# A layer with expert lookup on one core: the gates of the first token of each group of eight multiplied as high and low part

## The chip, the cores and the metric

The kernel runs on one core of a Trainium2 chip. The metric is the time of one execution on the device in microseconds. Times of single runs stand beside one profiled execution, in which every instruction has its start and duration.

## What is computed

One transformer layer for 256 tokens and 16 meta tokens, model width 1024: an input projection, sparse attention beside a pooling mixer, an output projection, and then the part that matters here, a product-key expert layer (PEER). Each token has 8 heads; each head picks 16 experts out of 128 x 128 with a softmax gate:

```python
    eid = jnp.take_along_axis(cand_i, pos, axis=-1)
    gate = jax.nn.softmax(top_s, axis=-1)
...
        a = jnp.einsum('td,tkd->tk', hb, peer_u[eb], preferred_element_type=jnp.float32)
        a = jax.nn.gelu(a, approximate=False)
        return jnp.einsum('tk,tkd->td', (gb * a).astype(hb.dtype), peer_v[eb])
```

So a token has 128 chosen experts, each with an index pair (i1, i2) and a gate.

## The kernel before

The kernel does not gather experts. It computes the products of all tokens with all 16,384 experts, in 128 blocks of 128, and multiplies them by a dense table of gates `gates[i2, i1, token]` that is zero where a token did not choose the expert. The stages are: the projections and attention (to about 150 us), the queries, the search for the best keys and the first "early" expert products (to about 254 us), the table of gates (about 259 to 340 us), and then 128 blocks in a steady rhythm of `up` and `down` products (to the end). The heavy products are made from float32 values split into a high and a low part in the type float32r, which TensorE takes in one pass; three such products (high x high, high x low, low x high) stand for one exact one. Products of plain float32 operands are called native here; TensorE shows two records (weight load and matmul) for each of them, and one for each single-pass product.

**The gate stage** is what the change touches. For one token the 128 x 128 table of gates is one product over its 128 choices: a one-hot matrix of one index against a one-hot matrix of the other index, each row of the latter multiplied by the choice's gate. Tokens are taken in 32 groups (NQ) of eight (GRP), q = 0 to 31, through OHS = 3 rotating slots:

- VectorE, `ones` (L1059): both one-hot matrices of eight tokens, by one comparison of 128 x 2048 elements against a row of numbers. It waits until TensorE has done group q - 3 (`b_done`).
- ScalarE, `gated` (L619), takes the first two tokens (ACT_T = 2): it multiplies the one-hot of 128 x 128 by the token's column of gates in `picks[:, 2]`, as the activation's scale, and writes plain float32 into `oh_g`. GpSimd, `gated` (L1277), does the same for the other six in one operation.
- TensorE, `gate_group` (L1574): waits for both (`ohg_up`, `ohp_up`) and for the copy of the slot's last results (`b_ev`), and makes eight native products of 128 x 128 x 128 into two banks of PSUM.
- ScalarE, `keep_gates` (L624): copies 128 x 1024 results into the table. It waits for `b_done` of that group, so in ScalarE's queue it stands behind the gated one-hots of the next group.

In the same stage seven more early expert products (13 to 19) are made by `split_part` (L1581) between the gate groups: a period of EARLY_Q = 4 groups holds 9 products after the group with q = 1 mod 4, 9 after q = 2 mod 4 and 6 after q = 3 mod 4. Each needs a block of expert weights split in halves: high part by ScalarE (`early_hi`, L636), low part by GpSimd (`early_lo`, L1285), and its result goes through a gelu on ScalarE (`early_gelu`, L566). The order of ScalarE's queue is written out by hand: in each iteration q the gated one-hots of q, then the copy of group q - 1; behind that, for q = 3 mod 4, the first half block, and for q = 0 mod 4 the gelu and the second half block. GpSimd takes its share of group q and then its half block (q = 0 and 1 mod 4). From q = 28 on no half blocks are left; at q = 29 ScalarE instead splits the first full block of the following stage (L560). The memory of the one-hots, `oh`, ends at element 8D of the row `rr` (D = 1024), and the last D elements, `g_sp`, are used only once all groups are done.

Of the kernel before, what the change touches and what calls it, by code (L numbers as in the profile page):

```python
# [8 lines left out]
ALU = mybir.AluOpType  # L9
ACT = mybir.ActivationFunctionType  # L10
AX = mybir.AxisListType
ds = bass.ds

P = 128
SEQ, META = 256, 16
T = SEQ + META
D = 1024
# [6 lines left out]
NK = 128  # L24
PH, TOPK = 8, 16
GRP = 8
NQ, OHS = SEQ // GRP, 3
# [4 lines left out]
ACT_T = 2  # L32
# [57 lines left out]
def layer(nc, x, meta, w_in, gq, gk, pool_w, w_out, wq, sk1, sk2, pu, pv, const, out):  # L90
    ctx = ExitStack()
    with ctx:
        def sb(name, shape, dt=F32):
            return ctx.enter_context(nc.sbuf_tensor(name, shape, dt))

        def sem(name):
            return ctx.enter_context(nc.semaphore(name))
# [4 lines left out]
        rr = sb("rr", [P, 9 * D], F32R)  # L102
# [4 lines left out]
        picks = sb("picks", [P, 3, SEQ])  # L107
        gel = sb("gel", [P, 2, SEQ])
        psum = ctx.enter_context(nc.psum_tensor("psum", [P, 8, 512], F32))
# [98 lines left out]
        ut = [rr[:, n:n + 2 * D].rearrange("p (a k n) -> p a k n", a=2, k=DK) for n in (0, 4 * D)]  # L208
        v_sp = [rr[:, n:n + 2 * D].rearrange("p (a d) -> p a d", a=2) for n in (6 * D, 2 * D)]
        oh = rr[:, 2 * D:8 * D].rearrange("p (s a q n) -> p s a q n", s=OHS, a=2, q=GRP)  # L210
        g_sp = rr[:, 8 * D:9 * D].rearrange("p (s a t) -> p s a t", s=2, a=2)

        def f(ap):
            return ap.bitcast(F32)
# [30 lines left out]
        ld_e = [sem(f"ld_e{s}") for s in range(2)]  # L245
        ld_v3 = sem("ld_v3")
        d_place, n_ev, ld_iota, a_root = sem("d_place"), sem("n_ev"), sem("ld_iota"), sem("a_root")
        d_inv, p_table = sem("d_inv"), sem("p_table")
        d_rel, p_qk = sem("d_rel"), sem("p_qk")
        p_cand, p_cide = sem("p_cand"), sem("p_cide")  # L250

# [33 lines left out]
        def early_bank(e):  # L285
            return (2, 5)[e % 2] if e < EARLY_TOP - 1 else 0
# [119 lines left out]
        def _(act):  # L406
# [155 lines left out]
            def early_gelu(e):  # L562
                act.wait_ge(e_up, e + 1)
                if e >= 2:
                    act.wait_ge(st_e[e % 2], 16 * (e // 2))
                act.activation(gel[:, e % 2, :], psum[:, early_bank(e), 0:SEQ], ACT.Gelu).then_inc(e_gel, 1)  # L566
# [45 lines left out]
            act.activation(picks[:, 0:2, :].rearrange("p a t -> p (a t)"), psum[:, 6, :], ACT.Copy).then_inc(pk_ev, 1)  # L612
            act.wait_ge(pe_pk, 2)
            act.activation(picks[:, 2, :], psum[:, 7, 0:SEQ], ACT.Copy).then_inc(pk_ev, 1)
            early_gelu(EARLY_TOP - 2)

            def gated(s, tok):
                for j in range(ACT_T):
                    i = act.activation(oh_g[:, s, j, :], f(oh[:, s, 1, j, :]), ACT.Copy, scale=picks[:, 2, ds(tok + j, 1)])  # L619
                i.then_inc(ohg_up, 1)  # L620

# [3 lines left out]
                   .then_inc(b_ev, 1)  # L625

            act.wait_ge(pk_ev, 2)

            def early_hi(j, half):
                e, ks = EARLY_TOP + j, slice(half * DK // 2, (half + 1) * DK // 2)  # L630
                act.wait_ge(ld_u[e % 2], 16 * (e // 2 + 1))
                if j and half == 0:
                    act.wait_ge(e_half, j)
                elif j:
                    act.wait_ge(e_up, e)
                act.activation(ut[0][:, 0, ks, :], u_raw[:, e % 2, ks, :], ACT.Copy).then_inc(e_hi, 1)  # L636

            for q in range(NQ):
                act.wait_ge(oh_up, q + 1)
                gated(q % OHS, GRP * q)  # L640
                if q == 1:
                    early_gelu(EARLY_TOP - 1)
                    early_hi(0, 0)
                    early_hi(0, 1)
                if q:
                    act.wait_ge(b_done, q)
                    keep_gates((q - 1) % OHS, GRP * q - GRP)
                if q % EARLY_Q == EARLY_Q - 1 and EARLY_TOP + q // EARLY_Q + 1 < EARLY:
                    early_hi(q // EARLY_Q + 1, 0)
                if q and q % EARLY_Q == 0 and EARLY_TOP + q // EARLY_Q - 1 < EARLY:  # L650
                    early_gelu(EARLY_TOP + q // EARLY_Q - 1)
                    if EARLY_TOP + q // EARLY_Q < EARLY:
                        early_hi(q // EARLY_Q, 1)
                if q == NQ - 3:
                    block_u(0, EARLY, 8 * EARLY + 16, True)
# [47 lines left out]
        def _(dve):  # L703
# [232 lines left out]
            for c in range(OUT0, WQ0):  # L936
                for t in range(2):
                    dve.wait_ge(z_done, z_after(c) - 1 + t)
                    n = (c - OUT0) * CW
# [118 lines left out]
            def ones(s, tok):  # L1058
                dve.tensor_tensor(oh[:, s], iota_in.unsqueeze(1).unsqueeze(1).to_broadcast([P, 2, GRP, NK]),  # L1059
                                  picks[:, 0:2, ds(tok, GRP)].unsqueeze(3).to_broadcast([P, 2, GRP, NK]), ALU.is_equal)\  # L1060
                   .then_inc(oh_up, 1)
# [3 lines left out]
            for q in range(NQ):  # L1065
                if q >= OHS:
                    dve.wait_ge(b_done, q - OHS + 1)
                ones(q % OHS, GRP * q)


            def block_v(s, b):
# [54 lines left out]
            for t in range(2):  # L1126
# [4 lines left out]
                for n in range(2):  # L1131
                    a = t * D + n * 512
# [163 lines left out]
        def _(pe):  # L1296
# [238 lines left out]
            for h in range(PH + 1):  # L1535
# [6 lines left out]
                if h != 2:  # L1542
                    g = h if h < 2 else h - 1
# [24 lines left out]
            def gate_group(q, s, first=False):  # L1568
                pe.wait_ge(ohg_up, q + 1)
                pe.wait_ge(ohp_up, q + 1)  # L1570
                if not first:
                    pe.wait_ge(b_ev, q - OHS + 1)
                for j in range(GRP):
                    i = pe.matmul(psum[:, 2 + 2 * s + j // 4, (j % 4) * P:(j % 4 + 1) * P], f(oh[:, s, 0, j, :]), oh_g[:, s, j, :],  # L1574
                                  start=True, stop=True)
                i.then_inc(b_done, 1)
# [12 lines left out]
            for q in range(NQ):  # L1589
                gate_group(q, q % OHS, q < OHS)  # L1590
                j, part = q // EARLY_Q, q % EARLY_Q
                e = EARLY_TOP + j
                if e < EARLY and part:
                    if part == 1:
                        pe.wait_ge(e_gel, e)
                    pe.wait_ge(e_lo, 2 * j + min(part, 2))
                    i = split_part(e, EARLY_K[part - 1], EARLY_K[part])
                    if part == 2:
                        i.then_inc(e_half, 1)
                    if part == 3:  # L1600
                        i.then_inc(e_up, 1)
# [92 lines left out]
```

## Time and profile before

| | us |
|---|---|
| median of 3 runs | 1002.54 |
| lowest and highest run | 1001.08, 1002.66 |
| the profiled execution | 1002.49 |
| its span, first to last instruction | 1000.5 |
| TensorE matmuls busy in the span | 978.5 |
| VectorE, ScalarE, GpSimd busy | 677.5, 442.3, 184.5 |

The profile names instructions by engine (PE is TensorE's matmul, PEld its weight loads, DVE VectorE, ACT ScalarE, POOL GpSimd, SP the queue of the loads and stores) and by the line of the kernel. TensorE's clock is granted in full in every slice of the span. Matmuls are pipelined, so their durations overlap: the distance from one start to the next is what a product costs, not the mean duration of one. Idle time in brackets stands behind an instruction that had to wait, with what released it.

### The profile page before, as it was taken

To read this page: it belongs to the slowest core of one execution; us is meant where nothing else is said; L and a number is where in the kernel's file an instruction comes from. 1 tells how busy PE (TensorE), PEld (TensorE's weight loads), DVE (VectorE), ACT (ScalarE), POOL (GpSimd) and SP (SyncE) were. 2 spreads that over 40 slices of the span, in tenths; PEclk is the share of its full clock that TensorE was granted. 3 is DMA by queue.
4 is the path that set the end of the run, shared out by engine and by line. 5 is a ranking of instruction groups with operands and counts; after the bars stand their busy time and mean duration, and the time that the engine had idled before them with its cause. 6 is when DMAs were issued, how large, how long until landed. Compare 5 with 4: busy or idle time off the path is not lost.

```text
span 1000.5 us, 18315 instructions
## 1 busy us (share of the span) xinstructions
PE 978.5 (98%) x6396; PEld 890.4 (89%) x6396; DVE 677.5 (68%) x1266; ACT 442.3 (44%) x698; POOL 184.5 (18%) x228
## 2 busy tenths in 40 slices
PE   7999899999999999999999999999999999999998
PEld 7898798887999878999999999999999999999997
DVE  5697737789888788565656565656565656565655
ACT  5555532212677633444444444444444444444442
POOL 3273304787678300000000000000000000000000
PEclk9999999999999999999999999999999999999999
DMA  7532136414412577545555555454555454555454
GB/s 243 180 119 96 56 114 206 142 56 141 121 54 80 161 237 244 185 170 206 172 207 170 207 171 206 171 206 170 207 173 205 172 205 171 199 179 206 171 203 151
DMA packets 69585, 168.34 MB, mean 168 GB/s; under 512 B 6688, under 2 KB 35488, under 8 KB 69552
## 3 DMA queue, kind: packets, MB, share of 16 engines
q1 hardware_dynamic: 68080, 167.47, 49.3%
q10 hardware_dynamic: 1472, 0.44, 0.2%
q8 instruction: 20, 0.33, 0.1%
q14 instruction: 13, 0.11, 0.0%
HBM read 163.16 MB, written 4.72 MB: 168 GB/s over the span
## 4 chain that ended last, share of the span: by engine, by line
PE 93%; DVE 3%; DMA 2%; ACT 1%; POOL 1%; issue 1%; DVEq 0%
PE psum L1311 38%; PE psum L1616 34%; PE psum L1574 6%; PE psum L1488 6%; PE psum L1524 4%; PE psum L1581 2%; DMA raw<-in_peer_u_dram 1%; PE psum L1518 1%; PE psum L1343 1%; POOL big L1196 1%; PE psum L1435 1%; PE psum L1303 0%; DVE big L750 0%; DVE big L873 0%; DMA cst<-in_const_dram 0%
## 5 line engine op out<-in xcount | busy, mean ns | idle before, releaser
L1616 PE MATMUL psum<-rr 128*128 128x512 f32 x1536 | 369.3, 391 | 1.1 <-issue 0.7
L1311 PEld LDWEIGHTS psum<-h_all,rr 128*128 128x128 f32 x2688 | 331.0, 188 | 8.9 <-DVE big L873 0.5
L1311 PE MATMUL psum<-h_all,rr 128*128 128x256 f32 (+1 forms) x2688 | 334.0, 280 | 0.1
L1616 PEld LDWEIGHTS psum<-rr 128*128 128x128 f32 x1536 | 280.7, 188 | 56.2 <-issue 0.9
L1073 DVE TENSOR_TENSOR rr<-raw,rr 128x1024 fp32r<-128x1024 f32 x109 | 133.5, 1225 | 215.5 <-ACT rr L664 215.5
L664 ACT ACTIVATE rr<-raw 128x1024 fp32r<-128x1024 f32 x109 | 115.6, 1061 | 287.2 <-PE psum L1616 287.2
L560 ACT ACTIVATE rr<-raw 128x1024 fp32r<-128x1024 f32 x108 | 114.6, 1061 | 54.6 <-DMA raw<-in_peer_u_dram 54.6
L1012 DVE TENSOR_TENSOR rr<-raw,rr 128x1024 fp32r<-128x1024 f32 x108 | 131.6, 1219 | 1.1 <-ACT rr L560 0.9
L1311 PE MATMUL psum<-rr,h_all 128*128 128x256 f32 (+1 forms) x672 | 81.3, 281 | 2.5 <-ACT raw L476 1.5
L1311 PEld LDWEIGHTS psum<-rr,h_all 128*128 128x128 f32 (+1 forms) x672 | 77.6, 175 | 5.5 <-issue 1.9
L1059 DVE TENSOR_TENSOR rr<-psum,picks 128x2048 fp32r<-128x2048 f32 x32 | 72.4, 2288 | 9.5 <-PE psum L1574 7.7
L1574 PE MATMUL psum<-raw,rr 128*128 128x128 f32 x512 | 62.9, 277 | 1.1 <-ACT raw L619 0.9
L1574 PEld LDWEIGHTS psum<-raw,rr 128*128 128x128 f32 x512 | 59.8, 192 | 2.7 <-ACT raw L619 2.1
L1088 DVE TENSOR_TENSOR rr<-big,rr 128x256 fp32r<-128x256 f32 x128 | 54.5, 426 | 4.4
L1488 PE MATMUL psum<-big 128*128 128x256 f32 x256 | 56.7, 379 | 0.0
L1082 DVE TENSOR_TENSOR big<-big,gel 128x256 f32 (+1 forms) x128 | 53.5, 418 | 4.5 <-ACT big L624 4.5
L1488 PEld LDWEIGHTS psum<-big 128*128 128x128 f32 x256 | 48.3, 190 | 6.4
L1277 POOL TENSOR_TENSOR raw<-rr,picks 128x768 f32<-128x768 f32 x32 | 47.9, 1499 | 21.7 <-DVE rr L1059 21.7
L1524 PE MATMUL psum<-big,raw 128*128 128x256 f32 x208 | 46.9, 381 | 1.2 <-DMA raw<-in_peer_u_dram 1.2
L1086 DVE TENSOR_SCALAR rr<-big 128x256 fp32r (+1 forms) x128 | 37.7, 294 | 13.7 <-PE psum L1616 3.7
L1524 PEld LDWEIGHTS psum<-big,raw 128*128 128x128 f32 x208 | 38.6, 190 | 7.4 <-DMA raw<-in_peer_u_dram 2.6
L624 ACT ACTIVATE big<-psum 128x1024 f32<-128x1024 f32 x32 | 32.8, 1024 | 18.9 <-PE psum L1574 18.3
(177 smaller groups left out, 723.1 us busy)
## 6 DMA issues: line engine op xcount, KB each, us to landing
raw<-in_peer_u_dram SPq DMA_DIRECT2D x128, 512.0 KB, 4.0
raw<-in_peer_v_dram SPq DMA_DIRECT2D x128, 512.0 KB, 3.5
big<-in_w_in_dram SPq DMA_DIRECT2D x10, 1024.0 KB, 5.5
big<-in_peer_wq_dram SPq DMA_DIRECT2D x8, 1024.0 KB, 5.6
big<-in_w_out_dram SPq DMA_DIRECT2D x4, 1024.0 KB, 5.1
up_kept<-gel SPq DMA_DIRECT2D x20, 128.0 KB, 3.7
gel<-up_kept SPq DMA_DIRECT2D x20, 128.0 KB, 3.5
big<-in_x_dram SPq DMA_DIRECT2D x2, 512.0 KB, 4.3
```

Source lines behind the costliest of these rows:

```text
L560: act.activation(ut[s][:, 0], u_raw[:, s], ACT.Copy).then_inc(ut_hi, 1)
L664: act.activation(v_sp[s][:, 0, :], v_raw[s], ACT.Copy).then_inc(v_hi, 1)
L1012: dve.tensor_tensor(ut[s][:, 1], u_raw[:, s], f(ut[s][:, 0]), ALU.subtract).then_inc(ut_lo, 1)
L1059: dve.tensor_tensor(oh[:, s], iota_in.unsqueeze(1).unsqueeze(1).to_broadcast([P, 2, GRP, NK]), picks[:, 0:2, ds(tok, GRP)].unsqueeze(3).to ...
L1073: dve.tensor_tensor(v_sp[s][:, 1, :], v_raw[s], f(v_sp[s][:, 0, :]), ALU.subtract).then_inc(v_lo, 1)
L1082: dve.tensor_tensor(gates_at(b), gates_at(b), act_in, ALU.mult).then_inc(d_g32, 1)
L1088: dve.tensor_tensor(g_sp[:, s, 1, :], gates_at(b), f(g_sp[:, s, 0, :]), ALU.subtract).then_inc(g_lo, 1)
L1311: i = pe.matmul(dst, lhs(a, k), rhs(b, k), start=(n == 0), stop=(n == 3 * DK - 1))
L1488: i = pe.matmul(query_out(c, a), wraw[:, c % 3, k, a * P:(a + 1) * P], t32[:, k, :], start=(k == 0), stop=(k == DK - 1))
L1524: i = pe.matmul(psum[:, early_bank(e), 0:SEQ], u_raw[:, e % 2, k, :], t32s[:, k, :], start=(k == 0), stop=(k == DK - 1))
L1574: i = pe.matmul(psum[:, 2 + 2 * s + j // 4, (j % 4) * P:(j % 4 + 1) * P], f(oh[:, s, 0, j, :]), oh_g[:, s, j, :], start=True, stop=True)
L1616: i = pe.matmul(psum[:, 4 + 2 * t + n, :], g_sp[:, s, x, t * P:(t + 1) * P], v_sp[s][:, y, n * 512:(n + 1) * 512], start=(first and m == 0 ...
```

## The change

The first token (j = 0) of each group is treated differently. Once, ahead of the groups, ScalarE copies the gates of these 32 tokens into float32r (`pk_hi`), and VectorE, after its first one-hots, subtracts them from the exact ones to get the low part (`pk_lo`). In each group ScalarE then makes two gated one-hots for token 0, one scaled by the exact gate and rounded by the write into float32r (the high part), one scaled by `pk_lo`, and one for token 1 as before: three activations in place of two. TensorE multiplies token 0 as two float32r products that accumulate into the same place of PSUM, and the other seven tokens natively as before. The new tiles lie in the last D elements of `rr`, which nothing else uses in this stage. ScalarE waits once for the low part ahead of its loop, VectorE once for the high part behind its first one-hots.

```diff
+        oh_s = rr[:, 8 * D:8 * D + 2 * OHS * NK].rearrange("p (s a n) -> p s a n", s=OHS, a=2)
+        pk_hi, pk_lo = (rr[:, n:n + NQ] for n in (8 * D + 2 * OHS * NK, 8 * D + 2 * OHS * NK + NQ))
...
             act.activation(picks[:, 2, :], psum[:, 7, 0:SEQ], ACT.Copy).then_inc(pk_ev, 1)
+            act.activation(pk_hi, psum[:, 7, 0:SEQ].rearrange("p (q g) -> p q g", g=GRP)[:, :, 0], ACT.Copy).then_inc(a_pick, 1)
             early_gelu(EARLY_TOP - 2)
 
             def gated(s, tok):
-                for j in range(ACT_T):
+                act.activation(oh_s[:, s, 0, :], f(oh[:, s, 1, 0, :]), ACT.Copy, scale=picks[:, 2, ds(tok, 1)])
+                act.activation(oh_s[:, s, 1, :], f(oh[:, s, 1, 0, :]), ACT.Copy, scale=f(pk_lo[:, tok // GRP:tok // GRP + 1]))
+                for j in range(1, ACT_T):
                     i = act.activation(oh_g[:, s, j, :], f(oh[:, s, 1, j, :]), ACT.Copy, scale=picks[:, 2, ds(tok + j, 1)])
                 i.then_inc(ohg_up, 1)
...
             act.wait_ge(pk_ev, 2)
+            act.wait_ge(d_pick_lo, 1)
...
                 ones(q % OHS, GRP * q)
+                if q == 0:
+                    dve.wait_ge(a_pick, 1)
+                    dve.tensor_tensor(pk_lo, picks[:, 2, :].rearrange("p (q g) -> p q g", g=GRP)[:, :, 0], f(pk_hi), ALU.subtract)\
+                       .then_inc(d_pick_lo, 1)
...
-                for j in range(GRP):
+                for a in range(2):
+                    pe.matmul(psum[:, 2 + 2 * s, 0:P], oh[:, s, 0, 0, :], oh_s[:, s, a, :], start=(a == 0), stop=(a == 1))
+                for j in range(1, GRP):
                     i = pe.matmul(psum[:, 2 + 2 * s + j // 4, (j % 4) * P:(j % 4 + 1) * P], f(oh[:, s, 0, j, :]), oh_g[:, s, j, :],
                                   start=True, stop=True)
```

## Rows read from the trace of the kernel before

**Rows 1.** The page: the chain that ended last, by line.

```profile
PE psum L1311 38%; PE psum L1616 34%; PE psum L1574 6%; PE psum L1488 6%; PE psum L1524 4%; PE psum L1581 2%; DMA raw<-in_peer_u_dram 1%; PE psum L1518 1%; PE psum L1343 1%; POOL big L1196 1%; PE psum L1435 1%; PE psum L1303 0%; DVE big L750 0%; DVE big L873 0%; DMA cst<-in_const_dram 0%
```

**Rows 2.** Busy time of each engine in one period of four groups.

```profile
279.92:290.15 10.23, 10.23 (x91) 10.05 (x90) 9.07 (x5) 7.84 (x16) 8.35 (x7) 1.00 0.23 64
```

**Rows 3.** Waits from 259 to 345 us: in total, times, longest.

```profile
ACT big L624 <- PE psum L1574: 18.3, 24, 1.3
...
PEld psum L1574 <- ACT raw L619: 2.1, 7, 1.0
```

**Rows 4.** Timeline of TensorE's weight loads over one period: start, length, operation, count.

```profile
281.69 1.86 PEld L1574 LDWEIGHTS psum<-raw,rr 128*128 128x128 f32 x16 [0.18 <-ACT raw L619]
...
284.53 1.86 PEld L1574 LDWEIGHTS psum<-raw,rr 128*128 128x128 f32 x16
...
287.38 1.87 PEld L1574 LDWEIGHTS psum<-raw,rr 128*128 128x128 f32 x16
...
289.17 0.78 PEld L1581 LDWEIGHTS psum<-h_all,rr 128*128 128x128 f32 x6
...
289.87 1.87 PEld L1574 LDWEIGHTS psum<-raw,rr 128*128 128x128 f32 x16
...
291.92 1.86 PEld L1574 LDWEIGHTS psum<-raw,rr 128*128 128x128 f32 x16 [0.18 <-ACT raw L619]
```

**Rows 5.** Timeline of ScalarE ahead of that last load, and line 619's group.

```profile
288.29 0.68 ACT L619 ACTIVATE raw<-rr,picks 128x128 f32<-128x128 f32 x2
...
289.48 1.02 ACT L624 ACTIVATE big<-psum 128x1024 f32<-128x1024 f32 x1 [0.51 <-PE psum L1574]
...
290.40 0.38 ACT L566 ACTIVATE gel<-psum 128x256 f32<-128x256 f32 x1
290.66 0.63 ACT L636 ACTIVATE rr<-raw 128x512 fp32r<-128x512 f32 x1
...
291.18 0.69 ACT L619 ACTIVATE raw<-rr,picks 128x128 f32<-128x128 f32 x2
...
L619 ACT ACTIVATE raw<-rr,picks 128x128 f32<-128x128 f32 x64 | 21.9, 392 | 2.5 <-DVE rr L1059 2.5
```

**Rows 6.** Single-pass products: loads at 256 and 512 moving columns; load forms (busy, mean).

```profile
57.43 25.14 PEld L1311 LDWEIGHTS psum<-rr,h_all 128*128 128x128 f32 x216 [0.88 <-ACT big L449]
...
343.28 8.05 PEld L1616 LDWEIGHTS psum<-rr 128*128 128x128 f32 x36 [0.91 <-issue]
...
L1311 PEld LDWEIGHTS psum<-rr,h_all 128*128 128x128 f32 x576 | 68.9, 188 | 3.7 <-issue 1.9 <-ACT big L449 0.9 <-POOL rr L1150 0.5
...
L1311 PEld LDWEIGHTS psum<-rr,h_all 128*16 128x16 f32 x96 | 9.0, 94 | 1.8
```

**Rows 7.** Timeline of VectorE and GpSimd early on, both with operands in SBUF.

```profile
18.64 4.60 POOL L1150 TENSOR_TENSOR rr<-big,rr 128x2048 fp32r<-128x2048 f32 x1 [9.41 <-ACT rr L419]
...
19.26 4.05 DVE L750 TENSOR_TENSOR big<-big 128x64 f32<-128x64 f32 x1 [2.46 <-ACT big L449]
...
23.24 0.18 DVE L752 TENSOR_TENSOR big<-big 128x32 f32<-128x32 f32 x1
```

**Rows 8.** Timeline at the start: GpSimd's shares of groups 1 and 2, TensorE's loads.

```profile
259.64 1.47 POOL L1277 TENSOR_TENSOR raw<-rr,picks 128x768 f32<-128x768 f32 x1 [0.66 <-DVE rr L1059]
...
261.23 1.86 PEld L1574 LDWEIGHTS psum<-raw,rr 128*128 128x128 f32 x16 [0.17 <-issue]
...
262.39 1.48 POOL L1277 TENSOR_TENSOR raw<-rr,picks 128x768 f32<-128x768 f32 x1
...
264.07 1.87 PEld L1574 LDWEIGHTS psum<-raw,rr 128*128 128x128 f32 x16
```

**Rows 9.** Timeline at the end: loads of groups 30 and 31, GpSimd's share of 31.

```profile
335.26 2.38 POOL L1277 TENSOR_TENSOR raw<-rr,picks 128x768 f32<-128x768 f32 x1 [1.03 <-DVE rr L1059]
335.49 1.86 PEld L1574 LDWEIGHTS psum<-raw,rr 128*128 128x128 f32 x16 [1.04 <-ACT raw L619]
...
337.71 1.86 PEld L1574 LDWEIGHTS psum<-raw,rr 128*128 128x128 f32 x16 [0.36 <-issue]
```

More of the change, by code:

```diff
@@ L247, in layer @@
         d_place, n_ev, ld_iota, a_root = sem("d_place"), sem("n_ev"), sem("ld_iota"), sem("a_root")
-        d_inv, p_table = sem("d_inv"), sem("p_table")
+        d_inv, p_table, a_pick, d_pick_lo = sem("d_inv"), sem("p_table"), sem("a_pick"), sem("d_pick_lo")
         d_rel, p_qk = sem("d_rel"), sem("p_qk")
```

## The prediction

> **What bounds the kernel now.** I began with the chain of the page [rows 1]: what ends last runs over TensorE nearly throughout. The changed line, L1574, holds 6% of it; the long terms, L1311 and L1616, are untouched. So everything is decided between about 259 and 340 us, where the 32 gate groups are multiplied.
>
> The busy time of a stretch there [rows 2] shows one period of four groups, 10.23 us: TensorE busy throughout, VectorE 9.07, ScalarE 7.84, GpSimd 8.35. By shares, ScalarE has 2.4 us of room. Shares do not tell where it lies, so I read the waits next [rows 3]: TensorE's weight loads waited for ScalarE's line 619 seven times, 2.1 us in all, the longest 1.0. In the timeline six of them are alike (0.18 us of idle, one per period, at 271.46 us and every 10.23 us on); the long one comes in the tail.
>
> The timeline of one period shows the place [rows 4, 5]. TensorE issues group B (q = 1 mod 4) at 281.69, C at 284.53, D at 287.38, the split products behind D at 289.17, group A at 289.87, and the next B at 291.92. D takes 1.79 us: 16 records of 0.112, or 0.224 us for one native 128x128x128 product. From A to B it takes 2.05, so B starts 0.26 late. ScalarE says why: D's end releases the copy of the gates (289.48, 1.02 us), then come the gelu (290.40), the half block's high part (290.66), and only then the two gated one-hots of B (291.18 to 291.87). B starts at 291.92. From D's end to B the path is ScalarE's, four steps without a gap.
>
> **The change, part by part.**
>
> *One more ScalarE operation in each group.* Two activations of 128x128 become three. A pair spans 0.68 to 0.69 us and one alone takes 0.392 [rows 5], so one more in the queue adds 0.294. Is it hidden? A's pair ends at 288.97 (288.29 + 0.68) and A starts at 289.87: 0.9 us of slack. C and D have more, since ScalarE there waits for TensorE ahead of its copies; these waits, 18 us in all [rows 3], are the cover. In front of B there is none: B already waits, so all of it goes on the path. Six such places: 6 x 0.294 = 1.76 us. B of the last period (q = 29) has no half block ahead of it and did not wait; by my count its last one-hot now ends within 0.1 us of its turn. Zero.
>
> *The last groups.* Group 30 waits for ScalarE too, starts at 335.49 [rows 9] and moves by 0.29. But group 31 starts at 337.71, right behind GpSimd's share (335.26 + 2.38 = 337.64), which hangs on group 28's end. Group 30 needs 1.79 us and ended at 337.28, so 0.4 us of gap takes up the 0.29. Zero; without GpSimd's cover, 0.3.
>
> *A native product replaced by two single passes.* Removed: 0.224 us per group. Added: two single-pass products with 128 moving columns. No row has that form, so I bound it. Lower end: with 256 columns 216 loads span 25.14 us, 0.116 each; with 512 columns 36 loads span 8.05, 0.225 each [rows 6]. The cost follows the columns, and half of 256 gives 0.06, or 0.12 a pair: 0.10 less than now. Upper end of the likely prices: 0.116 as with 256 columns, if something other than the columns sets it; 0.232 a pair, 0.01 more. I take 0.112, so that a pair costs what the native product does, for this reason: each product of either kind comes with a weight load of its own, even where neighbours share the stationary operand (the 6 split products behind D, of which pairs share it, have 6 loads [rows 4]). A 128-column load takes 188 ns in its record and a 16-column one 94 [rows 6]: 94 ns for 112 columns, so about 0.107 us of pure loading for 128. Under 256 moving columns that hides; under 128 it does not. The change keeps two loads where there were two. So TensorE's work stays: 0 us, with 0.10 less to 0.01 more per group as bounds, and a far worse price among the rivals.
>
> What a page makes of it: the Trainium skill, "TensorE: Matmul & The Clock Gate", section "LDWEIGHTS (loading the stationary operand)", gives columns / 1.2 in ns, 107 for 128 columns; this speaks against a gain from the change, and the difference of the two load rows agrees. Its section "Back-to-back issue gap" gives about 81 ns per load and matmul of 128 columns, which no row here shows; what the sum would be with that stands behind the first rival.
>
> *The high and low part, once.* ScalarE's copy of 128x32 is smaller than the 0.39 of rows 5 and runs while VectorE makes its first one-hots, for which ScalarE waits anyway: 0. VectorE waits for that copy behind its first one-hots (over 2 us each [rows 2]), so finds it done; its next one-hots queue behind the wait and the subtraction. A 128x32 tensor_tensor took 0.18 [rows 7], say 0.15 in the queue. The first gated one-hots of ScalarE wait for the low part, and the rest of its queue behind them; group 0 starts 1.79 us or more before group 1's 261.23 [rows 8] and VectorE's first one-hots end about 2.2 before 259.64, so some 2 us lie between, enough for the subtraction and three activations of 0.98: hidden. Not hidden is the second group: GpSimd's share ran from 259.64 to 261.11, group 1 started at 261.23. That costs 0.15. ScalarE's first half block is pushed by 0.15 + 0.3, GpSimd's low part behind it too, and its third share, done at 263.86 against group 2 at 264.07 [rows 8], passes its slack of 0.2 by some 0.25, of which 0.15 is in the shift already. Together 0.25 us once. Bounds: 0, and 1.5 if the subtraction is held up for a whole GpSimd share (1.47 us). No load or store is moved; the orders of SP and GpSimd stay.
>
> **Sum.** 1.76 + 0 + 0 + 0.25 = 2.0 us. The profiled execution took 1002.49 us (span 1000.5), 0.05 below the median of 1002.54. 1002.49 + 2.0 = 1004.5.
>
> **The rivals.**
>
> *The single passes follow the columns (0.06 each).* For it: the cost per column between 256 and 512 in rows 6. Against it: the two load rows. From D's end to B the path is ScalarE's, then it is TensorE's over B, C and D: 0.294 - 3 x 0.10, about 0 per period. A's saving only lengthens B's wait. Start and tail give back some 0.3 against their 0.25. Time: 1002.2 to 1002.5. So even at half the price the gain is eaten where ScalarE is late; 2 us faster would need ScalarE's extra hidden as well. By the page's 81 ns it would be 0.294 - 3 x 0.06 = 0.11 a period, 0.7 us in all, 1003.2. Chance 0.2.
>
> *A narrow single pass is no single pass (the other side).* If with 128 columns it streams as slowly as a native product, each costs 0.224, and the pair 0.45. Place: every gate group. In a period B, C and D each take 0.224 more; A's fits in B's wait of 0.55. That is 6 x (0.294 + 0.67) = 5.8, plus some eight groups at both ends, 1.8, plus 0.25: 7.8 us, 1010.3. It decides from about 0.116 per pass upwards, where TensorE begins to add to ScalarE's term. No row has fewer than 256 moving columns in this kind, so nothing excludes it; against it stand the equal price per column of 256 and 512, and a mechanism that I lack. Chance 0.12.
>
> *ScalarE's extra is hidden after all,* if the wait before B is not its own: +0.3, 1002.8. The 0.05 us between its end and B's start speaks against it. Chance 0.04.
>
> *VectorE's subtraction collides with GpSimd.* A 128x64 tensor_tensor started at 19.26, during a GpSimd operation from 18.64, and ended only with it, 4.05 us later [rows 7]. Here GpSimd starts after the one-hots' end, with the subtraction already under way. 1004.5 + 1.3 = 1005.8. Chance 0.04.
>
> **The numbers.** The forecast has the remaining 0.60: 1003.9 to 1005.2 by its small terms. About 0.2%, 2.0 us, is what a measurement of this kernel can tell from no change. The forecast lies on that line, so I halve its chance. Slower: 0.30 + 0.12 + 0.04, and 0.02 for terms I set at zero: 0.48. Same: 0.30 less that 0.02, 0.04, and 0.14 of the first rival: 0.46. Faster: its other 0.06. The range takes in the first rival and the collision and leaves out the narrow pass: 1002.0 to 1006.8.
>
> **What would show it.** A period of 10.52 us; three ScalarE one-hots spanning 0.98; TensorE's wait before B 0.3 longer, with C, D and A starting without any; a group still 1.79 us long, its first loads 0.112 apart. A group of 1.69 would be the first rival (period near 10.23), one of 2.0 the second (period near 11.2). If the period stayed at 10.23 with groups of 1.79, or waits appeared before C or D, my account of ScalarE's path would be wrong.

## The result and the profile after

The changed kernel takes 1004.28 us (median of 8 runs, 1003.49 to 1005.35) against 1001.59 for the kernel before in the same comparison (8 runs, 1000.7 to 1002.67). The ratio is 1.0027, with a 95% interval of 1.0018 to 1.0036: 1.8 to 3.6 us slower. The forecast was 1004.5. The profiled execution took 1003.76 us, with a span of 1001.6.

The spans of the two profiled executions differ by only 1.1 us, because in this one the gate stage happened to begin 0.90 us earlier (group 0's loads at 258.20, not 259.10). The change didn't do that: ScalarE's copy of the gates, which stands ahead of everything that was changed, already starts 0.88 us earlier (253.71, not 254.59). So the stages are compared from their own first load. From there to the first load of the next stage's `up` it was 80.40 us (259.10 to 339.50) and is 82.48 (258.20 to 340.68): 2.08 us more. What follows is the same again: 661.0 us before, 660.9 after.

One period of the changed kernel, TensorE's weight loads in the timeline (start, length, line, count; L1584 is the new pair, L1586 the seven native products, L1593 the split products). It answers to rows 4:

```profile
281.70 0.30 PEld L1584 LDWEIGHTS psum<-rr 128*128 128x128 f32 x2 [0.47 <-ACT raw L624]
281.92 1.64 PEld L1586 LDWEIGHTS psum<-raw,rr 128*128 128x128 f32 x14
283.48 1.13 PEld L1593 LDWEIGHTS psum<-h_all,rr 128*128 128x128 f32 x9
284.54 0.31 PEld L1584 LDWEIGHTS psum<-rr 128*128 128x128 f32 x2
...
287.39 0.30 PEld L1584 LDWEIGHTS psum<-rr 128*128 128x128 f32 x2
...
289.17 0.77 PEld L1593 LDWEIGHTS psum<-h_all,rr 128*128 128x128 f32 x6
289.88 0.31 PEld L1584 LDWEIGHTS psum<-rr 128*128 128x128 f32 x2
290.11 1.64 PEld L1586 LDWEIGHTS psum<-raw,rr 128*128 128x128 f32 x14
292.22 0.30 PEld L1584 LDWEIGHTS psum<-rr 128*128 128x128 f32 x2 [0.47 <-ACT raw L624]
```

B starts at 281.70 and again at 292.22: a period of 10.52 us in place of 10.23. Inside it a group still takes 1.78 us (281.70 to 283.48), the pair 0.22 of it (281.70 to 281.92), and D to the split products behind it 1.78. B to C, C to D and D to A are 2.84, 2.85 and 2.49 us; only A to B has grown, from 2.05 to 2.34. The idle time that the profile shows before B was 0.18 and is 0.47.

ScalarE over the same stretch, which answers to rows 5 (L621 and L622 are token 0's high and low one-hot, L624 token 1's):

```profile
289.48 1.02 ACT L629 ACTIVATE big<-psum 128x1024 f32<-128x1024 f32 x1 [0.22 <-PE psum L1586]
290.41 0.38 ACT L568 ACTIVATE gel<-psum 128x256 f32<-128x256 f32 x1
290.67 0.63 ACT L642 ACTIVATE rr<-raw 128x512 fp32r<-128x512 f32 x1
291.19 0.40 ACT L621 ACTIVATE rr<-rr,picks 128x128 fp32r<-128x128 f32 x1
291.48 0.40 ACT L622 ACTIVATE rr<-rr 128x128 fp32r<-128x128 f32 x1
291.77 0.40 ACT L624 ACTIVATE raw<-rr,picks 128x128 f32<-128x128 f32 x1
```

From D's end to B it is the same queue with one member more. The members start 0.29 apart, the last ends at 292.17 and TensorE starts B at 292.22. The busy times of this period and the waits of the stage (in total, times, longest) answer to rows 2 and 3:

```profile
281.70:292.22 10.52, 10.24 (x88) 10.05 (x89) 9.16 (x5) 8.90 (x20) 8.35 (x7) 1.00 0.23 65
```

```profile
ACT big L629 <- PE psum L1586: 12.6, 23, 1.0
...
PEld psum L1584 <- ACT raw L624: 4.1, 7, 1.3
```

ScalarE's busy time rose by 1.06 us per period (7.84 to 8.90), and still it is idle for 1.6 of 10.52. Its waits for TensorE, the cover of the prediction, fell from 18.3 to 12.6 us: 5.7 of the 9.4 us of added work (32 x 0.294) went in there. In front of B there was no such cover, and there TensorE's wait grew.

The 2.08 us of the stage by stretch, from first loads of both kernels:

| stretch | before | after | difference |
|---|---|---|---|
| group 0 to group 1 | 2.13 | 2.25 | +0.12 |
| group 1 to group 2 | 2.84 | 3.05 | +0.21 |
| group 2 to group 4 | 5.34 | 5.33 | 0 |
| group 4 to group 5 (A to the first late B) | 2.05 | 2.35 | +0.30 |
| group 5 to group 25, five periods | 51.15 | 52.60 | +1.45 |
| group 25 to the first `up` | 16.89 | 16.90 | 0 |

### The profile page after: what moved, and what is told of

It is laid out like the page before. It is cut to its first block, busy times and chain, and to the rows that moved or that the text cites. A ratio compares the mean times of both kernels' runs of the same rounds, so it can differ in the third digit from the quotient of the medians.

```text
span 1001.6 us, 18349 instructions
## 1 busy us (share of the span) xinstructions
PE 977.0 (98%) x6396; PEld 889.0 (89%) x6396; DVE 678.3 (68%) x1267; ACT 451.1 (45%) x731; POOL 184.7 (18%) x228
## 4 chain that ended last, share of the span: by engine, by line
PE 92%; ACT 3%; DMA 2%; DVE 2%; POOL 1%; issue 1%; SPq 0%; DVEq 0%; ACTq 0%
PE psum L1321 39%; PE psum L1628 34%; PE psum L1498 6%; PE psum L1586 4%; PE psum L1534 4%; PE psum L1593 2%; DMA raw<-in_peer_u_dram 1%; DMA big<-in_w_in_dram 1%; PE psum L1528 1%; PE psum L1584 1%; POOL big L1206 1%; PE psum L1445 1%; DVE big L879 0%; DVE big L887 0%; PE psum L1391 0%
## 5 line engine op out<-in xcount | busy, mean ns | idle before, releaser
L1586 PE MATMUL psum<-raw,rr 128*128 128x128 f32 x448 | 56.8, 278 | 0.0
L1586 PEld LDWEIGHTS psum<-raw,rr 128*128 128x128 f32 x448 | 52.6, 192 | 0.0
L681 ACT ACTIVATE gel<-psum 128x256 f32<-128x256 f32 x108 | 39.5, 366 | 1.5 <-PE psum L1321 1.5
```

## The experiments

Seven kernels. Each was profiled; all but one were also timed against the kernel before, whose medians in the two comparisons were 1002.06 and 1002.07.

**1. TensorE's part alone.** In the kernel before, token 0 becomes a single-pass pair, with no third one-hot and no low part.

```diff
-                for j in range(ACT_T):
+                act.activation(oh_s[:, s, 0, :], f(oh[:, s, 1, 0, :]), ACT.Copy, scale=picks[:, 2, ds(tok, 1)])
+                for j in range(1, ACT_T):
...
+                for a in range(2):
+                    pe.matmul(psum[:, 2 + 2 * s, 0:P], oh[:, s, 0, 0, :], oh_s[:, s, 0, :], start=(a == 0), stop=(a == 1))
+                for j in range(1, GRP):
```

> Token 0 as two single-pass products, but ScalarE makes only two one-hots per group: both products use the same rounded high part, so the low part of token 0's gates is left out and its high part counted twice. ScalarE-path theory: TensorE's pair costs 0.224 us like the native product and ScalarE's chain is the old one, so the period is 10.23 us and the time that of the kernel before within 0.3 us. Rival, TensorE's change of kind costs something itself: the period stays above 10.23 and the time 1 to 2 us above before.

Measured: 1001.88 us against 1002.06, ratio 0.9997 (0.9987 to 1.0007). Two periods' B in its trace, and the load before each:

```profile
278.20 0.31 PEld L1576 LDWEIGHTS psum<-rr 128*128 128x128 f32 x2
280.25 0.30 PEld L1576 LDWEIGHTS psum<-rr 128*128 128x128 f32 x2 [0.18 <-ACT raw L621]
...
288.43 0.31 PEld L1576 LDWEIGHTS psum<-rr 128*128 128x128 f32 x2
290.48 0.30 PEld L1576 LDWEIGHTS psum<-rr 128*128 128x128 f32 x2 [0.18 <-ACT raw L621]
```

The period is 10.23 (280.25 to 290.48), the wait before B is the old 0.18, A to B the old 2.05. The whole stage, from group 0 to the first `up`, takes 80.43 us against 80.40. So the change of kind on TensorE costs nothing and gives nothing.

**2. ScalarE's part alone.** In the kernel before, one more activation per group that nobody uses.

```diff
+                act.activation(oh_s[:, s, 0, :], f(oh[:, s, 1, 0, :]), ACT.Copy, scale=picks[:, 2, ds(tok, 1)])
                 for j in range(ACT_T):
```

> The kernel before with one more 128x128 activation per group whose result nobody uses; the eight native products stay. ScalarE-path theory: period 10.52 to 10.53 us (0.294 more), 6 x 0.294 = 1.8 us slower than before, 0.2 more at the start, so +1.8 to +2.1. Rival, ScalarE has 2.4 us of room per period and hides it: period 10.23, time as before.

Measured: 1003.97 us, ratio 1.0022 (1.0012 to 1.0031), so 1.9 us. Its B loads, all native, and the first groups:

```profile
258.61 1.96 PEld L1576 LDWEIGHTS psum<-raw,rr 128*128 128x128 f32 x16
260.75 1.86 PEld L1576 LDWEIGHTS psum<-raw,rr 128*128 128x128 f32 x16 [0.17 <-issue]
263.79 1.86 PEld L1576 LDWEIGHTS psum<-raw,rr 128*128 128x128 f32 x16
...
281.99 1.86 PEld L1576 LDWEIGHTS psum<-raw,rr 128*128 128x128 f32 x16 [0.47 <-ACT raw L621]
...
292.51 1.86 PEld L1576 LDWEIGHTS psum<-raw,rr 128*128 128x128 f32 x16 [0.47 <-ACT raw L621]
```

Period 10.52, wait 0.47: the changed kernel's numbers with none of its TensorE part. The start shows which term is whose: group 0 to 1 is 2.14 us, as before (no subtraction here), group 1 to 2 is 3.04, as in the changed kernel. So 0.21 of the start comes from the third one-hot and 0.12 from the subtraction.

**3. What sets the price of a narrow single-pass product.** In six groups, a row of equal products of one form, written over before they are read:

```diff
+                form = {6: (True, 64, 128), 8: (False, 128, 128), 12: (False, 64, 128), 16: (False, 128, 64), 20: (False, 64, 64), 24: (False, 128, 256)}.get(q)
+                if form:
+                    native, m, n = form
...
+                    for a in range(8 if native else 16):
+                        pe.matmul(psum[0:m, 2 + 2 * s, 0:n], f(row) if native else row, col, start=True, stop=True)
```

> The changed kernel with repeated products of one form added in six groups (16 single-pass ones of stationary x moving columns 128x128, 64x128, 128x64, 64x64, 128x256, and 8 native ones of 64x128), to read the distance from load to load. The weight load sets the price (0.107 us for 128 columns, 0.053 for 64): 128x128 and 128x64 both 0.11; 64x128 and 64x64 about 0.06; 128x256 0.116; native 64x128 0.112 per record, from its streaming. A fixed issue cost of about 0.11 per product: all single-pass forms but 128x256 at 0.11, 64x64 too. Cost by moving columns above some floor: 128x64 and 64x64 below 128x128 by the same amount.

Measured: 1011.2 us in one execution, with the added products; it serves only for the distances between loads. The loads of the single-pass rows, and of what comes behind each, in the order of the diff (stationary x moving columns 128x128, 64x128, 128x64, 64x64, 128x256; the shape in the line is the stationary operand's):

```profile
281.96 1.87 PEld L1589 LDWEIGHTS psum<-rr 128*128 128x128 f32 x16
283.76 0.30 PEld L1591 LDWEIGHTS psum<-rr 128*128 128x128 f32 x2
...
293.74 1.09 PEld L1589 LDWEIGHTS psum<-rr 128*64 128x64 f32 x16
294.75 0.30 PEld L1591 LDWEIGHTS psum<-rr 128*128 128x128 f32 x2
...
304.72 1.88 PEld L1589 LDWEIGHTS psum<-rr 128*128 128x128 f32 x16
306.52 0.30 PEld L1591 LDWEIGHTS psum<-rr 128*128 128x128 f32 x2
...
316.50 1.07 PEld L1589 LDWEIGHTS psum<-rr 128*64 128x64 f32 x16
317.48 0.30 PEld L1591 LDWEIGHTS psum<-rr 128*128 128x128 f32 x2
...
327.46 1.99 PEld L1589 LDWEIGHTS psum<-rr 128*128 128x128 f32 x16
329.38 0.31 PEld L1591 LDWEIGHTS psum<-rr 128*128 128x128 f32 x2
```

The clock was granted in full (1.00). From the first of 16 loads to the next line's: 1.80, 1.01, 1.80, 0.98 and 1.92 us, or 0.1125, 0.063, 0.1125, 0.061 and 0.120 each. Halving the moving columns changes nothing (0.1125 both times); halving the stationary ones takes the price from 0.1125 to 0.063, and with both halved it is 0.061. Only with 256 moving columns does the streaming come through. Native operands show the other limit: 16 records of 64 stationary and 128 moving columns,

```profile
274.75 1.72 PEld L1589 LDWEIGHTS psum<-raw,rr 128*64 128x64 f32 x16
```

have loads 0.106 us apart ((1.72 - 0.137) / 15, with 137 ns for one load), although they load half the columns. Here the price follows the moving columns: the native early products of the kernel before, with 256 of them, have loads twice as far apart, 0.216 us ((4.08 - 0.19) / 18).

```profile
254.99 4.08 PEld L1524 LDWEIGHTS psum<-big,raw 128*128 128x128 f32 x19
```

A single-pass product of 256 moving columns costs 0.116 to 0.120, so a native record costs per moving column about what two single passes would. That it streams its columns twice fits this, but no run looks inside a record. So a narrow single-pass product pays for its load; in a native record of 128 x 128 the load (0.1125) and the streaming (0.106) cost nearly the same; and two single passes cost one native product. A fixed issue cost of 0.11 and a cost by moving columns are both excluded as the limit of the single passes here.

**4. The wait before B taken away, in the kernel before.** The second half block's high part moves behind the copy of group A; GpSimd's low part moves behind its share of C.

```diff
                     early_gelu(EARLY_TOP + q // EARLY_Q - 1)
-                    if EARLY_TOP + q // EARLY_Q < EARLY:
-                        early_hi(q // EARLY_Q, 1)
+                if q > 1 and q % EARLY_Q == 1 and EARLY_TOP + q // EARLY_Q < EARLY:
+                    early_hi(q // EARLY_Q, 1)
...
-                if EARLY_TOP + j < EARLY and part in ((0, 1) if j else (1, 2)):
-                    early_lo(j, part if j else part - 1)
+                if EARLY_TOP + j < EARLY and part in ((0, 2) if j else (1, 2)):
+                    early_lo(j, part // 2 if j else part - 1)
```

> The kernel before with only the order changed: the second half block's high part goes behind the copy of group A in ScalarE's queue (so B's one-hots follow the gelu at once), and GpSimd takes its low part behind its share of C. ScalarE-path theory: TensorE no longer waits before B, the period is its own 9.97 us (10.23 less 0.26), 6 x 0.26 = 1.6 us faster than before. Rival, something else stands right behind ScalarE (VectorE's one-hots, GpSimd's share of C now late): period 10.1 or more, under 1 us faster.

Measured: 1000.43 us against 1002.06, ratio 0.9983 (0.9974 to 0.9993), 1.6 us faster. ScalarE and TensorE in its trace:

```profile
289.29 0.38 ACT L566 ACTIVATE gel<-psum 128x256 f32<-128x256 f32 x1
289.55 0.69 ACT L619 ACTIVATE raw<-rr,picks 128x128 f32<-128x128 f32 x2
290.86 1.02 ACT L624 ACTIVATE big<-psum 128x1024 f32<-128x1024 f32 x1 [0.62 <-PE psum L1574]
291.78 0.62 ACT L636 ACTIVATE rr<-raw 128x512 fp32r<-128x512 f32 x1
```

```profile
278.77:288.76 9.99, 9.99 (x91) 9.99 (x90) 9.07 (x5) 7.74 (x16) 8.37 (x7) 1.00 0.24 66
```

B's one-hots now end at 290.24, ahead of their turn, and ScalarE has 0.62 us to spare before it copies A. The period is 9.99, and the loads (the second column, PEld) fill it: TensorE has no gap. Of the 0.26 us by which B was late, 0.24 are gone (10.23 less 9.99), so they were ScalarE's order, and next to nothing stood behind it.

**5. The same order in the changed kernel.**

> The changed kernel with that same new order. ScalarE-path theory: with the half block out of the way the third one-hot is hidden before B too (chain from D's end 2.35 us against TensorE's 2.49), period 9.97 to 10.05 us in place of 10.52, so 3 us faster than the changed kernel and 1 us faster than before (the start still costs 0.33). Rival, ScalarE is short in total and another group waits instead: period 10.2 or more.

Measured: 1000.90 us against 1002.07, ratio 0.9987 (0.9978 to 0.9997).

```profile
289.09:299.10 10.01, 10.01 (x91) 10.01 (x89) 9.08 (x5) 8.90 (x20) 8.36 (x7) 1.00 0.24 67
```

With all three one-hots in place, ScalarE busy 8.90 us per period as in the changed kernel, the period is 10.01 and TensorE has no gap. ScalarE was never short in total; in this kernel's periods the third one-hot costs only where it stands in a queue that TensorE already waits for. Not much is to spare: B's last one-hot now ends at 290.87, 0.05 before B's first load (290.92). Against the kernel in 4 it has no advantage: 0.5 us more in the medians, 0.36 in the stage (79.30 against 78.94), which is the start's 0.33.

**6. The subtraction on GpSimd,** ahead of its loop, in the changed kernel.

```diff
             pool.wait_ge(pk_ev, 2)
+            pool.wait_ge(a_pick, 1)
+            pool.tensor_tensor(pk_lo, picks[:, 2, :].rearrange("p (q g) -> p q g", g=GRP)[:, :, 0], f(pk_hi), ALU.subtract)\
+                .then_inc(d_pick_lo, 1)
```

> The changed kernel with the low part's single subtraction on GpSimd, ahead of its loop, in place of VectorE behind its first one-hots. If the start's 0.33 us come from VectorE's next one-hots being late: the step from group 0 to group 1 falls from 2.25 to 2.13 us, and the step to group 2 stays at 3.0 to 3.05 because of the later half block; the time falls by 0.1 us, not to be told from the changed kernel. Periods stay at 10.52.

Measured: 1004.23 us, ratio 1.0019 (1.0009 to 1.0029) against before. In the trace:

```profile
258.66 0.41 PEld L1583 LDWEIGHTS psum<-rr 128*128 128x128 f32 x2
...
260.80 0.30 PEld L1583 LDWEIGHTS psum<-rr 128*128 128x128 f32 x2 [0.17 <-issue]
...
263.85 0.30 PEld L1583 LDWEIGHTS psum<-rr 128*128 128x128 f32 x2
```

Group 0 to 1 is 2.14 us, as before the change, and group 1 to 2 is 3.05, as in the changed kernel. So the 0.12 is VectorE's one-hots coming later by the subtraction, and the time itself cannot show it.

**7. The suspected cost doubled:** a fourth activation per group in the changed kernel.

```diff
+                act.activation(oh_g[:, s, 0, :], f(oh[:, s, 1, 0, :]), ACT.Copy, scale=picks[:, 2, ds(tok, 1)])
                 for j in range(1, ACT_T):
```

> The changed kernel with the suspected cost doubled: one more activation of 128x128 per group (token 0's plain gated one-hot, used by nobody). ScalarE-path theory: linear, period 10.81 to 10.82, 6 x 0.294 = 1.8 us slower than the changed kernel, up to 2.5 when C or A begins to wait too; 4 to 5 us slower than before. Rival, the first extra one only used up a slack at some other place: no clean 0.29 step.

Measured: 1006.47 us against 1002.07, ratio 1.0038 (1.0024 to 1.0053): 4.4 us above before.

```profile
282.98 0.30 PEld L1585 LDWEIGHTS psum<-rr 128*128 128x128 f32 x2 [0.76 <-ACT raw L625]
...
293.77 0.30 PEld L1585 LDWEIGHTS psum<-rr 128*128 128x128 f32 x2 [0.76 <-ACT raw L625]
...
304.58 0.30 PEld L1585 LDWEIGHTS psum<-rr 128*128 128x128 f32 x2 [0.76 <-ACT raw L625]
```

The wait before B goes 0.18, 0.47, 0.76 with two, three and four activations: 0.29 for each. The period is 10.79 to 10.81. The six places are not all of it, though. The stage is 2.38 us longer than in the changed kernel (84.86 against 82.48): some 1.7 in front of the six B, 0.28 more from group 0 to group 2, and 0.44 more behind group 28 (334.33 to 343.48, 9.15 in place of 8.71), where the profile now shows idle time before groups 29 and 31 too, 0.24 and 0.21. What hid the third activation at the end no longer hides the fourth; the expectation had allowed for more than the six places, with up to 2.5 us.

## Why the prediction held, point by point

**ScalarE's path before B.** 6 x 0.294 = 1.76 us was forecast; the trace shows 0.30 + 1.45 = 1.75, all before B. Experiments 2 and 7 make it with ScalarE's operation alone, one step of 0.29 each; experiment 5 makes it vanish by order alone, and experiment 4 does so with the wait that was there before.

**TensorE's exchange at no cost.** Forecast 0.112 us per single pass, by the difference of two load records. The changed kernel has 0.22 for the pair, experiment 1 shows no change in the time, and experiment 3 shows that the stationary columns set the price. By the section "LDWEIGHTS (loading the stationary operand)" of the Trainium skill's "TensorE: Matmul & The Clock Gate" a load takes columns / 1.2 in ns, 107 for 128 columns and, as an estimate by that formula, 53 for 64. The distances here are 112.5 and 61 to 63, so the trace agrees within some 5 to 10 ns that lie beside the load. The 81 ns of its section "Back-to-back issue gap" do not hold for these float32r products: the measurement decides, at 112.5. Both rivals on TensorE's price, 0.06 and 0.224 per pass, are excluded; a price near the lower one came only with half the stationary columns, not with half the moving ones.

**The start.** 0.25 us forecast, 0.33 measured. The subtraction was put at 0.15 in the queue and costs 0.12; it took 0.20 in its record and the next one-hots began 0.12 after its start (256.39 and 256.51), so GpSimd did not hold it up. GpSimd's third share was put 0.1 past its slack beyond that shift; it is 0.21.

```profile
256.39 0.20 DVE L1077 TENSOR_TENSOR rr<-picks,rr 128x32 fp32r<-128x32 f32 x1
256.51 8.87 DVE L1065 TENSOR_TENSOR rr<-psum,picks 128x2048 fp32r<-128x2048 f32 x4
...
261.91 1.48 POOL L1287 TENSOR_TENSOR raw<-rr,picks 128x768 f32<-128x768 f32 x1
...
263.50 0.30 PEld L1584 LDWEIGHTS psum<-rr 128*128 128x128 f32 x2
```

The share ends at 263.39, and group 2 starts 0.11 later. The forecast counted the slack from the share's end to group 2's load, 0.2, and left out this 0.11, which lies between the two in any case; only 0.09 of slack was there, against 0.30 by which the share came later behind group 1's first load. ScalarE's and GpSimd's first shares were hidden, as forecast.

**The tail.** Forecast zero. Group 28's first load to the next stage's `up` is 8.71 us in both kernels (330.79 to 339.50, 331.97 to 340.68), with group 30 coming 0.29 later in between. GpSimd's share of group 31 takes it up: it ends at 338.82 and group 31 starts at 338.89, 6.92 behind group 28's first load as before. The B of q = 29 was forecast within 0.1 us of its turn; its last one-hot ends at 333.75 and the group starts at 333.79, at no cost.

**The sum.** 2.0 us forecast, 2.08 in the stage, 2.7 in the medians with an interval from 1.8 to 3.6. The other 0.6 us has no place in the trace. The stage of every kernel, from group 0's first load to the first `up`, beside its median:

| kernel | stage | against before | medians, against before |
|---|---|---|---|
| before | 80.40 | | |
| changed | 82.48 | +2.08 | +2.7 |
| 1, TensorE's part | 80.43 | +0.03 | -0.2 |
| 2, ScalarE's part | 82.34 | +1.94 | +1.9 |
| 4, before, new order | 78.94 | -1.46 | -1.6 |
| 5, changed, new order | 79.30 | -1.10 | -1.2 |
| 6, low part by GpSimd | 82.35 | +1.95 | +2.2 |
| 7, four activations | 84.86 | +4.46 | +4.4 |

In the experiments the two columns agree within some 0.2 us; only the changed kernel is off. Its own comparison had a lower median for the kernel before, 1001.59, where the two later ones, with 25 and 20 runs, had 1002.06 and 1002.07. The eight runs behind it lie in two clusters, four from 1000.70 to 1001.08 and four from 1002.10 to 1002.67, and their median falls between them. Against the later medians the change costs 2.2 us. So some 0.5 of the 0.6 us most likely comes from the eight runs of the kernel before, and not from the change; the changed kernel was not timed again, so this isn't shown.

That the forecast of 1004.5 comes so close to 1004.28 is in part luck: it started from 1002.49, 0.9 above the median of 1001.59, and this makes up for the 0.7 by which 2.0 falls short of 2.7. The 2.08 us of the stage and its parts are what bears the forecast out. As to no change or slower, on the line of 0.2%: the ratio of 1.0027 lies beyond it, and its interval begins just below, at 1.0018.

## What to carry to other kernels

A busy share does not say whether an engine can take more work: find the place in its queue where another engine already waits, and price the new instruction there at its full step in the queue (0.294 us here, not the 0.392 of its record), and elsewhere at nothing as long as the slack holds; experiment 7 shows where it ends. Such a place is also where time can be had: here the order of one half block in two queues was worth 1.5 us in the stage, while the exchange on TensorE gave nothing. And before native products are exchanged for single-pass ones, compare the weight load with the streaming: at 128 stationary and 128 moving columns, two single passes cost what one native float32 product does.

## What the runs showed of the hardware

Below the price of the weight load the moving columns had practically no effect here: 128 and 64 of them cost 0.1125 us each with 128 stationary columns (1.80 us for 16, both times), and 0.063 and 0.061 with 64. One single-pass product of 256 moving columns costs 0.120, hardly more than one of 128, so by estimate a high and a low part side by side under one load would take about half of the pair's 0.225; its two results would have to be added up elsewhere, and this was not tried.
